# Half of the low-rank products of the RWKV stage computed at the end of the output stage ahead of it

## What is computed

```python
x = layer_norm(ALPHA * x + y @ w_out, ln_g, ln_b)            # end of the first block, layer 1
h = _modulate(_rmsnorm(x, norm1_g), shift, scale)            # begin of the second
z = h @ w_in                                                 # its last columns: 32 + 32 + 96 low-rank ones
z = z + (_token_shift(z) - z) * mu
w_log = -softplus(-(w0 + tanh(xw) @ w2)) - 0.5               # xw: 32 columns (decay)
a = sigmoid(a0 + xa @ a2)                                    # xa: 32 columns
g = sigmoid(xg) @ g2                                         # xg: 96 columns (gate)
```

## Time and profile before

| | us |
|---|---|
| median of 3 runs | 2926.93 (2925.25 to 2927.55) |
| profiled execution, its time | 2926.73 |
| its span, first to last instruction | 2925.0 |
| TensorE busy | 2796.2 (96%) |
| VectorE busy | 1756.6 (60%) |
| ScalarE busy | 1271.4 (43%) |
| POOL busy | 562.4 (19%) |
| mean granted TensorE clock, share of full | 0.986 |

### The profile page before, as it was taken

How to read it: one execution, slowest core, us unless ns; L and a number is a source line. 1 busy time by engine, 2 the same in 40 slices (tenths; PEclk the granted TensorE clock), 3 DMA queues, 4 the chain that set the end, 5 groups by cost and what they waited for, 6 DMA issues and landing times. The chain is left out here.

```text
span 2925.0 us, 48206 instructions
## 1 busy us (share of the span) xinstructions
PE 2796.2 (96%) x19709; PEld 2170.2 (74%) x19709; DVE 1756.6 (60%) x2526; ACT 1271.4 (43%) x2051; POOL 562.4 (19%) x383
## 2 busy tenths in 40 slices
PE   8999999999999999999999989998799999999997
PEld 6877767777777777777756576678678788888884
DVE  2332163685566666666425354353885899999995
ACT  2111020222454554453323222232443788888883
POOL 2222132222322222213231010101000111111102
PEclk9999999999999999999999999999799999999999
DMA  5111211754222221113221020113663799999997
GB/s 176 40 40 47 86 66 58 216 190 129 59 58 58 59 58 53 56 47 120 73 71 41 24 69 23 62 62 129 199 230 153 299 395 395 401 393 390 397 388 285
DMA packets 232144, 445.60 MB, mean 152 GB/s; under 512 B 18256, under 2 KB 160096, under 8 KB 206608
## 3 DMA queue, kind: packets, MB, share of 16 engines
q1 hardware_dynamic: 224896, 426.07, 41.0%
q0 software_dynamic: 7056, 16.79, 1.6%
HBM read 389.78 MB, written 61.94 MB: 154 GB/s over the span
## 5 line engine op out<-in xcount | busy, mean ns | idle before, releaser
L1223 DVE TENSOR_TENSOR fox_pT_lo<-psum,fox_pT_hi 128x512 fp32r<-128x512 f32 (+2 forms) x192 | 107.0, 557 | 179.3 <-ACT fox_pT_hi L1162 169.9
L1030 PE MATMUL psum<-x_hi,w_hi 128*128 128x512 f32 x512 | 210.8, 412 | 2.3 <-PEq L100 1.7
L1032 PE MATMUL psum<-x_hi,w_lo 128*128 128x512 f32 x512 | 200.9, 392 | 0.0
L1031 PE MATMUL psum<-x_lo,w_hi 128*128 128x512 f32 x512 | 200.2, 391 | 0.0
L3162 POOL DMA_INDIRECT xg<-n_rows,idx x33 | 84.1, 2549 | 476.7 <-PE psum L3049 454.9
L1733 PE MATMUL psum<-hT,wr 128*128 128x512 f32 x384 | 167.1, 593 | 0.0
L3272 DVE TENSOR_TENSOR lo_g<-land_g,hi_g 128x2048 fp32r<-128x2048 f32 x68 | 152.8, 2288 | 16.8 <-ACT hi_g L3198 16.8
L1173 ACT ACTIVATE fox_p<-fox_p,fox_bias 128x256 f32<-128x256 f32 (+7 forms) x128 | 99.6, 778 | 118.2 <-DVE fox_bias L1209 114.8
L3272 DVE TENSOR_TENSOR lo_u<-land_u,hi_u 128x2048 fp32r<-128x2048 f32 x66 | 150.4, 2282 | 0.0
L3272 DVE TENSOR_TENSOR lo_d<-land_d,hi_d 128x2048 fp32r<-128x2048 f32 x64 | 143.5, 2283 | 0.0
L181 PE MATMUL psum<-x_hi,w_hi 128*128 128x512 f32 x352 | 138.4, 393 | 0.0
(11 more groups left out here) (564 smaller groups left out, 7325.2 us busy)
## 6 DMA issues: line engine op xcount, KB each, us to landing
land_g<-in_moe_w_gate SPq DMA_DIRECT2D x66, 1024.0 KB, 7.5
land_u<-in_moe_w_up SPq DMA_DIRECT2D x66, 1024.0 KB, 7.5
land_d<-in_moe_w_down SPq DMA_DIRECT2D x64, 1024.0 KB, 8.2
ada<-in_ada_w SPq DMA_DIRECT2D x24, 1024.0 KB
y_slots<-yb SPq DMA_DIRECT2D x33, 512.0 KB, 9.4
w<-in_w_in SPq DMA_DIRECT2D x27, 512.0 KB, 6.5
wo<-in_w_out SPq DMA_DIRECT2D x12, 1024.0 KB, 9.9
w_land<-in_w_kv_shared SPq DMA_DIRECT2D x23, 512.0 KB, 4.1
```

Source lines behind the costliest of these rows:

```text
L1030: nc.tensor.matmul(bank[:], hi[:, d, :], E.x_hi[:, d, cols], start=(d == 0), stop=False)
L1031: nc.tensor.matmul(bank[:], hi[:, d, :], E.x_lo[:, d, cols], start=False, stop=False)
L1032: last = nc.tensor.matmul(bank[:], lo[:, d, :], E.x_hi[:, d, cols], start=False, stop=(d == ND - 1))
```

## The change

In the second output stage (`modulate`) the two runs of identity products give way to two groups of low-rank products for tokens 0 to 511: the 64 columns ahead of the last turn, the 96 behind it. They go to the first two banks that `ringD` of that stage hands out after the tiles: banks 0 and 1. SP's load of `w_lora` moves ahead of the store of the last tile. In the RWKV stage the rings swap their banks, so that the first two of `ringD` are banks 0 and 1; TensorE takes them as filled and forms only tokens 512 to 1023. ScalarE and VectorE go through the four banks in another order: both groups' first halves, then both second halves. `stage_out` of layer 0 keeps its identity products.

```diff
@@ stage_out, tensor
-                keep_warm(nc, E, pe, ringD, 30 if modulate else 14)
-                turn(NT - 1)
-                keep_warm(nc, E, pe, ringD, 10)
+
+                def low_rank_ahead(i):
+                    bank, free = ringD.take(("lora", i))
+                    wait(pe, ringD.free, free)
+                    lo, n = LORAS[i]
+                    for d in range(ND):
+                        last = nc.tensor.matmul(bank[0:n, :], E.w_lora[:, d, lo:lo + n], E.xT[:, d, 0:HALF], start=(d == 0), stop=(d == ND - 1))
+                    last.then_inc(E.lora_ahead, 1)
+
+                if modulate:
+                    pe.wait_ge(E.w_lora_landed, 16)
+                    pe.wait_ge(ringA.free, ringA.nth(("t", NT // 2 - 1, 1)))
+                    low_rank_ahead(0)
+                    turn(NT - 1)
+                    low_rank_ahead(1)
+                else:
+                    keep_warm(nc, E, pe, ringD, 14)
+                    turn(NT - 1)
+                    keep_warm(nc, E, pe, ringD, 10)
@@ stage_out, sync
                 for t in range(NT):
+                    if layer == 1 and t == NT - 1:
+                        sp.wait_ge(whole_used, 1)
+                        sp.dma_start(E.w_lora[:], win[:, :, 2 * GW + 3 * RW:2 * GW + 3 * RW + 2 * LORA + GATE_LORA]).then_inc(E.w_lora_landed, 16)
                     sp.wait_ge(rows_set, t + 1)
                     sp.dma_start(rows_out[t * P:(t + 1) * P, :], xs[t % NX][:]).then_inc(stored[t % NX], 16)
...
-                else:
-                    win = A["w_in_2"][0].rearrange("(c p) n -> p c n", p=P)
-                    sp.wait_ge(whole_used, 1)
-                    sp.dma_start(E.w_lora[:], win[:, :, 2 * GW + 3 * RW:2 * GW + 3 * RW + 2 * LORA + GATE_LORA]).then_inc(E.w_lora_landed, 16)
@@ stage_rwkv_pairs
-        ringA = Ring(E.banks[0:4], E.sem("rwA_full"), E.sem("rwA_free"))
-        ringD = Ring(E.banks[4:8], E.sem("rwD_full"), E.sem("rwD_free"))
+        ringA = Ring(E.banks[4:8], E.sem("rwA_full"), E.sem("rwA_free"))
+        ringD = Ring(E.banks[0:4], E.sem("rwD_full"), E.sem("rwD_free"))
@@ stage_rwkv_pairs, tensor
-                    pe.wait_ge(E.w_lora_landed, 16)
+                    for i in range(len(LORAS)):
+                        take(ringD, ("lora", i, 0))
+                    pe.wait_ge(E.lora_ahead, len(LORAS))
+                    pe.sem_inc(ringD.full, len(LORAS))
                     for i, (lo, n) in enumerate(LORAS):
-                        for hf in range(NH):
+                        for hf in range(1, NH):
@@ stage_rwkv_pairs, scalar
-                    for i, (_, n) in enumerate(LORAS):
-                        to = (xwa, E.xg)[i]
-                        for hf in range(NH):
+                    for hf in range(NH):
+                        for i, (_, n) in enumerate(LORAS):
+                            to = (xwa, E.xg)[i]
@@ stage_rwkv_pairs, vector
-                    for i, (n, to) in enumerate(((2 * LORA, xwa), (GATE_LORA, E.xg))):
-                        shifted(to, n, mu_x[i][:], [ringD.bank(("lora", i, hf)) for hf in range(NH)], 2 * i)
+                    tiles = [(2 * LORA, xwa, mu_x[0][:]), (GATE_LORA, E.xg, mu_x[1][:])]
+                    for i, (n, to, m) in enumerate(tiles):
+                        dve.wait_ge(S_["kept"], len(LORAS) + i + 1)
+                        link(dve, with_m(to, n, m, inside[0], ringD.bank(("lora", i, 0)), inside[1]))
+                        with_m(to, n, m, edge[0], ringD.bank(("lora", i, 0)), edge[1]).then_inc(ringD.free, 1)
+                    for i, (n, to, m) in enumerate(tiles):
+                        with_m(to, n, m, next_inside[0], ringD.bank(("lora", i, 1)), next_inside[1]).then_inc(ringD.free, 1)
```

More of the change, by code:

```diff
@@ L772, in _ @@
                     load_x(t)
+                win = A["w_in_2"][0].rearrange("(c p) n -> p c n", p=P)
                 for t in range(NT):
+                    if layer == 1 and t == NT - 1:
+                        sp.wait_ge(whole_used, 1)
+                        sp.dma_start(E.w_lora[:], win[:, :, 2 * GW + 3 * RW:2 * GW + 3 * RW + 2 * LORA + GATE_LORA]).then_inc(E.w_lora_landed, 16)
                     sp.wait_ge(rows_set, t + 1)
@@ L1494 @@
 LORA, GATE_LORA = 32, 96
+LORAS = ((0, 2 * LORA), (2 * LORA, GATE_LORA))
 DECAY = math.exp(-0.5)
@@ L1632, in stage_rwkv_pairs @@
         ka1 = cols[:, 32:36]
-        LORAS = ((0, 2 * LORA), (2 * LORA, GATE_LORA))
         mu_x = [E.sb(f"mu_x{i}", [n, 1], ctx=st) for i, (_, n) in enumerate(LORAS)]
@@ L2182, in _, with with_m @@
                 link.n = E.chain_n
+                def with_m(to, n, m, cols, bank, of_bank):
+                    return nc.vector.scalar_tensor_tensor(to[:, cols], bank[0:n, of_bank], m, to[:, cols], ALU.mult, ALU.add)
+                inside, edge, next_inside = ((slice(1, HALF), slice(0, HALF - 1)), (slice(HALF, HALF + 1), slice(HALF - 1, HALF)),
+                                             (slice(HALF + 1, S), slice(0, HALF - 1)))
                 def shifted(to, n, m, banks, kept):
-                    V = nc.vector
-                    with_m = lambda cols, bank, of_bank: V.scalar_tensor_tensor(to[:, cols], bank[0:n, of_bank], m, to[:, cols], ALU.mult, ALU.add)
                     dve.wait_ge(S_["kept"], kept + 1)
-                    link(dve, with_m(slice(1, HALF), banks[0], slice(0, HALF - 1)))
+                    link(dve, with_m(to, n, m, inside[0], banks[0], inside[1]))
                     dve.wait_ge(S_["kept"], kept + 2)
-                    with_m(slice(HALF, HALF + 1), banks[0], slice(HALF - 1, HALF)).then_inc(ringD.free, 1)
-                    with_m(slice(HALF + 1, S), banks[1], slice(0, HALF - 1)).then_inc(ringD.free, 1)
+                    with_m(to, n, m, edge[0], banks[0], edge[1]).then_inc(ringD.free, 1)
+                    with_m(to, n, m, next_inside[0], banks[1], next_inside[1]).then_inc(ringD.free, 1)
                 def lora():
-                    for i, (n, to) in enumerate(((2 * LORA, xwa), (GATE_LORA, E.xg))):
-                        shifted(to, n, mu_x[i][:], [ringD.bank(("lora", i, hf)) for hf in range(NH)], 2 * i)
+                    tiles = [(2 * LORA, xwa, mu_x[0][:]), (GATE_LORA, E.xg, mu_x[1][:])]
[5 more added lines that the diff above has]
+                        with_m(to, n, m, next_inside[0], ringD.bank(("lora", i, 1)), next_inside[1]).then_inc(ringD.free, 1)
                 def proj(c, kind):
@@ L3558, in build_program @@
         E.w_lora_landed = E.sem("w_lora_ahead_landed")
+        E.lora_ahead = E.sem("lora_ahead")
         E.cx_landed = [E.sem(f"cx_landed{t}") for t in range(NT)]
```

## The result

The median of three runs is 2906.85 us (2906.40 to 2907.27) against 2926.93 (2925.25 to 2927.55): ratio 0.993, interval 0.9914 to 0.9946, 20.1 us faster. The forecast was 2914.9, in 2912.3 to 2918.3: right in direction, 8 us short. The three runs of before turned out to be no fair sample of it: in 60 executions on four occasions it took 2918.9 to 2935.5, mean 2927.3; the changed kernel took 2899.3 to 2910.1 in 13, mean 2904.4. Measured once more beside 19 executions of before, the ratio is 0.9918 (0.9902 to 0.9935). So the change is worth some 23 us on average, eleven more than the prediction's sum.

What follows compares the result with a forecast made beforehand. The prediction took TensorE as the bound, busy in 2796.2 of 2925.0 us. Its terms, -13.7 - 1.85 + 3.6 = -12.0 us, gave 2914.7 for the profiled execution and 2914.9 against the median, range 2912.3 to 2918.3.

Steps and rivals of the forecast that it cites:

- Part 1: RWKV stage: 32 of the 64 low-rank products leave, at 0.429 us each, saving 13.7 us.
- Part 2: Begin of the RWKV stage: the clock's fall goes away with shorter idle time, gaining 1.85 us, between 0 and 1.85.
- 1.0 lies on the side of 1.23: RWKV stage's begin: clock fell after 1.86 us idle, not after 1.23; at about 1.0 the fall was taken as gone.
- Part 3: Ahead of the last turn: 16 low-rank products replace 60 identity instructions, 6.86 us each way; no cost if `w_lora` is there.
- Part 4: Behind the last turn: 16 long products make TensorE finish last; the RWKV stage begins 3.6 us later, between 3.4 and 3.8.
- Part 5: RWKV stage: ScalarE and VectorE order, swapped rings and one more semaphore cost nothing, being covered.
- The sum at the seam: Output stage to first projection: -13.7 - 1.85 + 3.6 = -12.0 us, first projection at 1516.5 in place of 1528.57.
- All that follows in the stage hangs on TensorE's products and moves with them.: RWKV stage behind the first projection: everything moves with the products; later stages move too, as they begin at barriers.
- The sign that was to catch an error here: First projection to the span's end, 1396.4 us before: growth by more than 2 us would show the prediction wrong.

Runs made afterwards that it cites:

- the half change: Changed kernel with only the 64-column group ahead of the last turn, 10 identity products behind it and the 96-column group in the RWKV stage; 2910.9 us.
- plus_96: Kernel before with its last 10 identity products of 128x128 at the seam replaced by 34 of 64x64, 96 instructions more; 2917.5 us against 2927.3, ratio 0.9969.
- again_before: The kernel before, unchanged, executed once more for its trace; 2920.6 us in this one execution.

## Why the prediction was right, and where it failed

**Part 1, the products taken out (13.7 us): right.** 32 instructions left the stage. Begin to first projection is 14.15 us; the prediction has 13.9.

**Part 2, the clock at the begin (1.85 us): right in the two traces compared, wrong as a fixed sum.** The granted clock is 1.00 from 1501.2 on, and in all six traces with the short idle time (0.83 to 0.86 us) behind low-rank products or their padding there was no fall at the begin. The fall's size is 1.65 us (29.54 with it, 27.89 without), a little under the 1.85 of the sum. But "1.0 lies on the side of 1.23" took idle time as the thing that decides. Of the three traces with the old seam two have a fall (after 2.07 us both times) and one has none (after 2.05); 1.72 us passed without one in the half change; and in plus_96 the clock fell after 0.83 us, with 4 us of 64x64 products ahead. What the Trainium skill (TensorE: Matmul & The Clock Gate, Part 1) says, and the prediction set beside the sum, agrees with this: the same kernel shows different slow stretches from run to run. That the monitor runs free of the kernel no run here shows by itself. Single executions of one kernel lie 11 to 17 us apart, and they go with the clock: the fastest of before (2918.9) had a mean granted clock of 0.989, the slowest (2935.5) 0.982. The 2.3 us between three runs that I took as the size of such luck was itself luck.

**Part 3, nothing for the replaced identity products: right within 0.3 us.** The load was issued at 1477.75, landed in 4.5 us, 3 ahead of need. The last turn starts 7.01 us after the first low-rank product in place of 6.78 after the first identity product, against a zero.

**Part 4, the later begin (3.6 us): right, 3.7.** From TensorE's last product to the begin took 0.85 us in place of 1.01.

**Part 5, nothing for order and banks: right.** Tanh and sigmoid end at 1521.4, the first bank of r is read after, nothing waits; the weights landed at 1510.6, ahead of 1515.4; the banks alone are 1.0004.

**The sum at the seam: 12.0 forecast, 11.6 measured**, and 5.3 of 7.1 in the run that puts the stream back. That close hit rests on an execution of before that had the fall. Against again_before, which had none, the way from the begin of the output stage to the first projection takes 173.9 us in place of 183.8, 10.0 us less: the sum without part 2.

**The step that failed** is the sentence behind the sum: "All that follows in the stage hangs on TensorE's products and moves with them." The rest of the stage did not only move, it shrank by 5.7 us in the first pair of traces, and over all traces by 6 to 13 (503 to 506 us in the changed kernel, 512 to 516 where the edges stand as before). In its place the runs showed waits for the instruction stream, 21 to 23 us in all with the old edges and 12 with the new ones. I counted the 160 instructions as time and not as places in a stream. The sign that was to catch an error here looked for growth alone: the distance from the first projection to the end of the span, 1396.4 us, became 1389.7. The rows were there to see: five waits of TensorE of about 2 us released by "issue", in the view of waits that I had open, at a stage where the engine is the bound. No rival of mine had them, and the range left no room for a term of that kind. The rest of the 8 us missed is the fall at 1342 (1.6 us ahead of the seam) and 1.1 us in the later stages, less the 0.4 by which the seam fell short. The fall at 1342 isn't the code's doing: the second execution of the changed kernel has it, the second of before doesn't. The range was also added up wrongly: its own terms give 2913.0 to 2917.6 (0.2 and 1.7 down, 1.85, 0.2 and 0.6 up), not 2912.3 to 2918.3. Neither holds the result.

## What to carry to other kernels

Where TensorE is the bound and runs of short products follow each other, look for single waits of about 2 us that nothing but "issue" releases, and count the instructions between them: if the counts are multiples of 256 (or one off), any edit ahead of them that isn't a multiple too can be worth or cost several us by itself, and an A/B of such an edit needs a second version with the stream put back in place. Filler products are not free where they hide no time: they take places in the stream, and here the kernel was 8 us faster without their 160 instructions. And three runs that agree are no measure of the spread; 60 executions were 17 us apart.

## What the runs showed of the hardware that I had not expected

Waits for the instruction stream stand at exact multiples of 256 instructions (or one off), up to 2.6 us each, in TensorE's dense stretches. They end 1.2 to 1.7 us behind the end of a 16 KB transfer. The five long ones of before came back at the same places in all four traces with these edges; the changed kernel's one of 1.97 us was 0.28 in its second execution and 1.96 in its third. The clock fell behind some of them; where a fall's cost could be measured, at the stage's begin, it was 1.65 us. Identity products of 64x64 in a row took 0.06 us for each product instruction of the trace (4.88 us for 80); the kernel's own take a quarter of that in their dense runs (64 of line 1795 in 0.98 us, from 1976.44 in the kernel before). The clock may fall or not in the same place of the same kernel: after 2.05 us without a product it stayed at 2.4 GHz, after 2.07 it went to 1.2 (again_before and before).
